# Strassen over 12 instead of 8 of 16 chunks in the projections of a streaming attention layer, with two operand sums held in DRAM

## The chip, the core and the metric

The kernel runs on one core of a Trainium2 chip. The metric is the device time of one execution in microseconds, as the median of the runs.

## What is computed

One layer for two request groups, 592 tokens in all (16 meta tokens, 512 of a new stream, 64 of a running one): a combined input projection, two kinds of attention in 8 head pairs each, gates, an output projection, and a layer norm.

```python
def in_proj(h, w_in, b_f):
    z = jnp.einsum('bld,dc->blc', h, w_in)          # d = 2048
    fq, fk, fv, fg, ff, sq, sk, sv, sg = jnp.split(z, idx, axis=-1)
    lf = jax.nn.log_sigmoid((ff + b_f).astype(jnp.float32))

def mix_prompt(h, w_in, b_f, sinks, rel_bias, w_out):
    fq, fk, fv, fg, lf, sq, sk, sv, sg = in_proj(h, w_in, b_f)
    fo = fox_prompt(fq, fk, fv, lf) * jax.nn.silu(fg)
    so = swa_prompt(sq, sk, sv, sinks, rel_bias) * jax.nn.silu(sg)
    out = jnp.einsum('blc,cd->bld', jnp.concatenate([fo, so], axis=-1), w_out)

hp = layer_norm(ALPHA * hp + out_p, ln_g[l], ln_b[l])
```

`mix_sample` does the same for the running stream with cached keys and values. Everything is float32 in and out.

## The kernel before

**Precision.** A float32 operand is split in a high part (ScalarE's copy to the type fp32r) and a low part (VectorE's subtraction). A product is three matmuls: high by high, high by low, low by high.

**Tiles.** The input projection has 52 output tiles of 128 columns; their inner dimension of 2048 is 16 chunks of 128. x lies in SBUF as `xh` and `xl`, in two halves of 296 tokens (`HALF`), "early" and "late". Two tiles make a duo, which is one step: values and gates ("vg"), queries and keys ("qk"), or gates and queries ("gq"). Duo 0 is done plainly in the opening, duos 1 to 25 are the steps.

**Strassen.** In a step the 2 by 2 blocks are (two tiles) by (two halves of the tokens), with the inner dimension split in `first_x` and `second_x` of `CUT` = 4 chunks each. Seven products (`block_product`) take the place of eight; the other eight chunks are done plainly (`plain`). Three sums of x (numbers 7, 6 and 3, high and low, `sum7_high` and so on) are made once in the opening and stay in SBUF; a fourth, the difference of two late blocks, replaces the first chunks of `xh`, `xl`. The sums of weights are made anew in each step, for the next one: `make_seven`, `make_five`, `make_six`, and `make_four` within the step. Tile 1's and tile 0's weights come in `FRONT` (the 2 x `CUT` chunks) and `BACK`.

**Units and order.** A step is 15 units of 12 matmuls each (`UNITS`, function `unit`), 180 in all. Units 0, 1, 2, 3, 6, 7, 10 are the products; 4, 5 plain work of tile 0, early; 8, 9 of tile 1, early; 11, 12 of tile 0, late; 13, 14 of tile 1, late. The order on every engine is written by hand: each of `tensor`, `scalar`, `vector` walks the same list of places s (15 for each duo of a `Stretch`) and has its own table of what comes at which unit. Attention of the pair before is put between the units by `score_at`, `turn_at` and `value_at`: for each of 5 query tiles the scores (PE), row terms and maximum (DVE, `scores`), exp (ACT, `probabilities`), reciprocal (DVE), scaling (ACT, `scale_rows`), transposes (PE, `turn`), their copy (ACT, `keep_turned`), values (PE, `values`). A first stretch has duo 1 alone; then come stretches of two duos with one pair of attention, and six of one "gq" duo with one pair each. Engines wait on semaphores in the order of their list, so what stands behind a waiting instruction waits too.

**Evacuation.** `keep_first` (ACT) copies product 0; `take_six`, `take_seven`, `take_five` (DVE) build partial results; `join` adds them to a PSUM bank and `evacuate` and `split` make the high and low parts of q and k or the silu of the gates. A bank is free for the next step when `join` has read it (`corner_summed`, `side_summed`, `top_summed`, `bottom_summed`).

**DMAs.** SyncE's queue loads the weights of the next step: its two `FRONT` parts after `right_low` and `four_made`, `BACK` after `back_low`. GpSimd's queue stores keys, values and gated results, loads the cached ones, and copies the relative bias: `copy_bias` writes 128 copies of a row per head (`rel_copies`), so that `load_bias` can read it shifted.

**Opening.** The matmuls of duo 0 run while x arrives; ScalarE and VectorE split it, then VectorE makes the sums, the front parts and weight sums of duo 1, the forget gates (`gate_inputs`, `gate_ones`, then in step 1 a reciprocal, the logs and the running sums) and the silus of duo 0.

**End.** After duo 25 come 16 tiles of the output projection, whose operands are reloaded from `mix_rows` in parts (`MIX_PARTS`), and the layer norm.

## Time and profile before

| what | value |
|---|---|
| median of 3 runs | 1019.48 us (1019.35 to 1020.27) |
| profiled execution, its time | 1019.1 us |
| profiled execution, its span | 1017.6 us |
| mean granted TensorE clock | 0.996 of full |
| busy: TensorE, VectorE, ScalarE, GpSimd | 998.6, 715.2, 531.7, 81.5 us |
| DMA moved | 115.06 MB, 113 GB/s |
| step of a two-duo stretch, twice | 59.7 us |
| step of a gq duo | 31.4 us |

A busy time is the union of an engine's instructions. "PEld" is TensorE's weight load, which overlaps the matmuls. A chain row gives the start, the length and the work that the end of the program followed from; an "x36" behind it is the number of instructions merged.

### The profile page before, as it was taken

How to read it: one execution, taken by the hardware profiler on the slowest of the kernel's cores; microseconds unless marked ns; L12 is line 12 of the kernel's file. 1: busy time of each engine (PE TensorE's matmuls, PEld its weight loads, DVE VectorE, ACT ScalarE, POOL GpSimd, SP SyncE). 2: the span in 40 equal slices, each digit the busy share in tenths (PEclk: the TensorE clock that was granted, in tenths of full speed). 3: DMA queues.
4: the chain of work that ended last, by engine and by line, in shares of the span. 5: the costliest groups of instructions: out<-in, count | busy, mean ns of one | idle time of the engine just before them, and what ended most of it. 6: DMA issues, size and time to landing. Idle time of an engine off the chain costs nothing.

```text
span 1017.6 us, 20277 instructions
## 1 busy us (share of the span) xinstructions
PE 998.6 (98%) x7283; PEld 937.3 (92%) x7283; DVE 715.2 (70%) x1423; ACT 531.7 (52%) x1217; POOL 81.5 (8%) x156
## 2 busy tenths in 40 slices
PE   9999999999999999999999999999999999999995
PEld 6899999999999999999999999999999888888884
DVE  6988686776868677686767787668787655141685
ACT  5556465565645556464655676556677562111400
POOL 1620101001010100001010000000000000000000
PEclk9999999999999999999999999999999999999998
DMA  9142333223233323234321222231226443222423
GB/s 347 57 134 100 117 112 130 90 96 108 94 125 110 126 67 103 98 106 140 111 95 60 91 81 98 98 105 56 85 82 249 173 175 104 83 82 82 166 68 118
DMA packets 36258, 115.06 MB, mean 113 GB/s; under 512 B 9312, under 2 KB 9728, under 8 KB 33584
## 3 DMA queue, kind: packets, MB, share of 16 engines
q1 hardware_dynamic: 24208, 87.00, 24.8%
q0 software_dynamic: 11856, 27.14, 7.9%
q8 instruction: 31, 0.51, 0.2%
q10 hardware_dynamic: 144, 0.26, 0.1%
q14 instruction: 19, 0.16, 0.1%
HBM read 99.31 MB, written 18.29 MB: 116 GB/s over the span
## 4 chain that ended last, share of the span: by engine, by line
PE 86%; DVE 6%; DMA 4%; issue 2%; ACT 2%; SPq 1%; DVEq 0%; ACTq 0%
PE ps L1642 28%; PE ps L1652 25%; PE ps L1895 20%; PE ps L1860 5%; PE ps L1834 4%; DMA w_raw<-in_w_all 2%; PE ps L1818 2%; PE ps L1817 2%; DMA x_raw<-in_xT 2%; DVE wl L1118 1%; DVE tb L1295 1%; PE ps L1880 1%; SPq L582 0%; PE ps L1838 0%; ACT pt L961 0%
## 5 line engine op out<-in xcount | busy, mean ns | idle before, releaser
L1642 PE MATMUL ps<-xh,wh 128*128 128x296 f32 (+1 forms) x860 | 258.8, 301 | 0.2 <-DVE xl L1366 0.2
L1642 PE MATMUL ps<-xh,wl 128*128 128x296 f32 (+1 forms) x860 | 254.8, 296 | 0.0
L1642 PE MATMUL ps<-xl,wh 128*128 128x296 f32 (+1 forms) x860 | 254.6, 296 | 0.0
L1895 PE MATMUL ps<-wh,mix_parts 128*128 128x512 f32 x576 | 184.1, 390 | 0.0
L1642 PEld LDWEIGHTS ps<-xh,wh 128*128 128x128 f32 x860 | 161.8, 188 | 3.8 <-DVE xl L1366 1.8
L1642 PEld LDWEIGHTS ps<-xl,wh 128*128 128x128 f32 x860 | 161.9, 188 | 0.0
L1642 PEld LDWEIGHTS ps<-xh,wl 128*128 128x128 f32 x860 | 161.5, 188 | 0.0
L1118 DVE TENSOR_TENSOR wl<-w_raw,wh 128x1024 fp32r<-128x1024 f32 (+1 forms) x150 | 143.0, 953 | 19.8 <-ACT wh L853 8.5
L939 ACT ACTIVATE tb<-tb,small 128x256 f32<-128x256 f32 (+5 forms) x160 | 81.3, 508 | 92.2 <-DVE small L1314 64.2
L1895 PEld LDWEIGHTS ps<-wh,mix_parts 128*128 128x128 f32 x576 | 108.2, 188 | 22.3
L1895 PE MATMUL ps<-wl,mix_parts 128*128 128x512 f32 x320 | 124.5, 389 | 0.0
L1652 PE MATMUL ps<-xh,wh 128*128 128x296 f32 x400 | 121.4, 304 | 2.0 <-ACT first_part L891 1.4
L1652 PE MATMUL ps<-xl,wh 128*128 128x296 f32 x400 | 119.2, 298 | 0.0
L1652 PE MATMUL ps<-xh,wl 128*128 128x296 f32 x400 | 119.1, 298 | 0.0
L1652 PE MATMUL ps<-sum_high,wh 128*128 128x296 f32 x300 | 92.1, 307 | 1.2 <-DVE kT L1224 1.2
L1652 PE MATMUL ps<-sum_high,wl 128*128 128x296 f32 x300 | 89.7, 299 | 0.0
L1652 PE MATMUL ps<-sum_low,wh 128*128 128x296 f32 x300 | 89.6, 299 | 0.0
L1114 DVE TENSOR_TENSOR wl<-w_raw,wh 128x1024 fp32r<-128x1024 f32 x32 | 38.1, 1222 | 68.9 <-ACT wh L841 68.8
L1652 PEld LDWEIGHTS ps<-xh,wh 128*128 128x128 f32 x400 | 75.2, 188 | 2.6 <-ACT first_part L891 1.6
L951 ACT ACTIVATE tb<-tb,small 128x256 f32<-128x256 f32 (+4 forms) x160 | 71.7, 495 | 9.8 <-DVE small L1329 9.8
L1652 PEld LDWEIGHTS ps<-xl,wh 128*128 128x128 f32 x400 | 75.4, 189 | 0.0
L1652 PEld LDWEIGHTS ps<-xh,wl 128*128 128x128 f32 x400 | 75.2, 188 | 0.0
(198 smaller groups left out, 1737.3 us busy)
## 6 DMA issues: line engine op xcount, KB each, us to landing
w_raw<-in_w_all SPq DMA_DIRECT2D x106, 512.0 KB, 4.5
w_raw<-in_w_all SPq DMA_DIRECT2D x14, 1024.0 KB, 4.8
cbc<-c_rows POOLq DMA_DIRECT2D x16, 360.0 KB, 4.1
x_raw<-in_xT SPq DMA_DIRECT2D x7, 592.0 KB, 11.7
rows<-in_x_p POOLq DMA_DIRECT2D x4, 1024.0 KB, 5.2
out_y_p<-rows SPq DMA_DIRECT2D x16, 256.0 KB, 2.5
mix_rows<-mixT POOLq DMA_DIRECT2D x14, 288.0 KB, 2.4
rel_copies<-rel_rows POOLq DMA_DIRECT2D x8, 384.0 KB, 10.5
```

Of the source, the lines that this page charges most:

```text
L939: nc.scalar.activation(t, t, ACT.Exp, bias=nm, accum_out=total[:, i % 3, head:head + 1]).then_inc(exp_done, 1)
L951: nc.scalar.activation(row, row, ACT.Copy, scale=recip[:, i % 3, head:head + 1]).then_inc(scaled, 1)
L1114: nc.vector.tensor_tensor(wl[slot][:, a], w_raw[slot % 2][:, a], wh[slot][:, a].bitcast(F32), ALU.subtract).then_inc(w_low, 1)
L1118: nc.vector.tensor_tensor(low, raw, high.bitcast(F32), ALU.subtract).then_inc(done, 1)
L1295: ins = nc.vector.scalar_tensor_tensor(out=rows_[:, head, a:b], in0=st.score_out(ps, head, piece, b - a), scalar=cqp[:, i, head:head + 1], ...
L1642: ins = nc.tensor.matmul(ps[:, bank, result(tile, h)], a[f][:, w], b[:, ko, first:first + width], start=(ko == n_first and i == 0), stop=( ...
L1652: ins = nc.tensor.matmul(ps[:, bank, 0:HALF], a[:, w], b[:, j, :], start=(start and j == 0 and i == 0), stop=(stop and j == CUT - 1 and i ...
L1817: nc.tensor.matmul(out, queries, k2[:, head, a:b], start=True, stop=False)
L1818: ins = nc.tensor.matmul(out, queries, k_low[:, head, a:b], start=False, stop=True)
L1834: ins = nc.tensor.transpose(st.turn_out(ps, head, j), tb[:, i % SLOTS, head, first:first + P], ident[:])
L1860: ins = nc.tensor.matmul(ps[head_rows(head), bank, at:at + q], v_nat[:, block_, HD * head:HD * head + HD], moving[:, head, 0:q], start=(j ...
L1895: ins = nc.tensor.matmul(ps[:, bank, :], a, b[slot][:, w], start=(ko == 0 and i == 0), stop=(ko == KO - 1 and i == len(products) - 1))
```

## The change

`CUT` becomes 6 chunks, so Strassen covers 12 of 16 and `REST`, 2 chunks a unit, is done plainly. A step is 29 pieces of 6 matmuls (`PIECES`, `UNIT_PIECES`), and every table of every engine is written anew in pieces; the distances of attention double with them (`lag`). Units 8 to 12 change their order: the late half of tile 0 (product 8, plain 9 and 10) now comes before the plain work of tile 1's early half (11, 12). The sums 6 and 3 no longer both lie in SBUF: they share `sum_both`. In the opening sum 6 is stored to DRAM (`sum_rows`), sum 3 is made in place of an x block and split in step 1 (`last_sum`), then stored too; in every later step SyncE fetches sum 6 after unit 7 and sum 3 after unit 1. Before the first front loads of step 2 SyncE waits for both stores. The front loads of duo 1 wait for `w_low` 3 and 4 instead of 1 and 2. The silus of duo 0 use other buffers, the gate terms lie elsewhere with one tile fewer, and the logarithm moves into step 1. `rel_copies` holds 32 copies a head instead of 128, and `load_bias` reads it in four parts.

```diff
 UNITS = 15
+UNIT_PIECES = [3, 3, 3, 3, 1, 1, 3, 3, 3, 1, 1, 1, 1, 1, 1]
+PIECES = sum(UNIT_PIECES)
 DUOS = PROJ_TILES // 2
-CUT = KO // 4
+CUT = 3 * KO // 8
+REST = (KO - 2 * CUT) // 2
-GATES_TURNED_AT, V_FIRST_AT = 11, 14
+GATES_TURNED_AT, V_FIRST_AT = 22, 28
-BIAS_COPIES = FOX_PAIRS
+BIAS_COPIES, COPIES = FOX_PAIRS, CHUNK // 2
-MIX_PARTS = [(0, 2), (2, 5), (5, 8), (8, 12), (12, 14)]
+MIX_PARTS = [(0, 2), (2, 6), (6, 9), (9, 12), (12, 14)]
...
         elif len(duos) == 2:
-            score = [3 * i + 3 for i in range(5)]
+            score = [6 * i + 6 for i in range(5)]
         else:
-            score = [2 * i + 1 for i in range(5)]
-        turn = [x + 4 for x in score]
+            score = [4 * i + 2 for i in range(5)]
+        self.lag = 1 if final else 2
+        turn = [x + 4 * self.lag for x in score]
...
-        sum7_high, sum7_low, sum6_high, sum6_low, sum3_high, sum3_low = (
-            sb(f"sum{n}", [P, CUT, HALF], F32R) for n in ("7_high", "7_low", "6_high", "6_low", "3_high", "3_low"))
+        sum7_high, sum7_low = (sb(f"sum{n}", [P, CUT, HALF], F32R) for n in ("7_high", "7_low"))
+        sum_both = sb("sum_both", [P, 2, CUT, HALF], F32)
+        both_high, both_low = (sum_both[:, i, :, :].bitcast(F32R) for i in range(2))
...
@@ block.sync
             for f in range(2):
-                sp.wait_ge(w_low, f + 1)
+                sp.wait_ge(w_low, f + 3)
                 load_part(1, f, FRONT, front_loaded)
             for f in range(2):
-                sp.wait_ge(w_low, f + 3)
                 load_part(1, f, BACK, back_loaded)
+            sp.wait_ge(sum_low, 2)
+            sp.dma_start(sum_rows[0], sum_both[:].rearrange("p a b c -> p (a b c)")).then_inc(sums_stored, 16)
             sp.wait_ge(back_low[0], 1)
             load_part(2, 0, BACK, back_loaded)
+            sp.wait_ge(sum_low, 4)
+            sp.dma_start(sum_rows[1], sum_both[:].rearrange("p a b c -> p (a b c)")).then_inc(sums_stored, 16)
+            sp.wait_ge(sums_stored, 32)
...
-                sp.wait_ge(*((four_made, d) if f == 0 else (right_low, d)))
+                sp.wait_ge(*((four_made, d) if f == 0 else (five_low, d)))
...
+            def load_sums(i, used, loaded):
+                sp.wait_ge(unit_done, used)
+                sp.dma_start(sum_both[:].rearrange("p a b c -> p (a b c)"), sum_rows[i]).then_inc(loaded, 16)
+            def load_three(d):
+                load_sums(1, UNITS * (d - 1) + 2, three_loaded)
+            def load_duo(d):
+                load_next_front(d, 0)
+                load_next_front(d, 1)
+                load_next_back(d)
+                load_sums(0, UNITS * (d - 1) + 8, six_loaded)
+                sp.wait_ge(back_low[0], d + 1)
+                load_part(d + 2, 0, BACK, back_loaded)
...
@@ block.scalar, per place
+                        if r == 3:
                             keep_first(st, k)
+                        if r == 4:
                             five_part(d, (unit_done, st.after(k, 0)))
+                        if r == 6:
                             right_part(d, (unit_done, st.after(k, 1)))
+                        if st.first and r == 7:
+                            last_sum(st)
+                        if r == 24 and not last:
+                            seven_part(d + 1, (unit_done, st.after(k, 8)))
+                            six_part(d + 1, (unit_done, st.after(k, 7)))
...
+                    if inside and r == 18 and not last:
+                        front_parts(d + 1, (unit_done, st.after(k, 6)))
...
@@ block.vector, per place
+                        if r == 6:
                             take_six(st, k)
+                            five_part(d)
+                        if r == 8:
+                            right_part(d)
+                        if r == 9:
                             take_seven(st, k)
+                            make_four(d, (unit_done, st.after(k, 2)))
+                        if r == 14:
                             join(st, k, 0, 0)
+                        if r == 17:
                             take_five(st, k)
+                        if r == 25:
+                            join(st, k, 0, 1)
+                        if r == 27:
                             join(st, k, 1, 0)
...
+                            if r == 20:
                                 front_parts(d + 1)
+                            if r == 21:
                                 make_seven(d + 1, (unit_done, st.after(k, 7)))
                                 make_five(d + 1)
+                            if r == 22:
                                 make_six(d + 1)
+                            if r == 25:
                                 seven_part(d + 1)
                                 six_part(d + 1)
+                            if r == 28:
                                 back_parts(d + 1, 0)
...
@@ block.tensor, unit()
                 elif u == 1:
+                            pe.wait_ge(six_loaded, 16 * d - 16)
...
                 elif u == 7:
+                            pe.wait_ge(three_loaded, 16 * d - 16)
```

## Rows read from the trace of the kernel before

**Rows 1.** The page: engines, busy us (share of the span) xinstructions.

```profile
PE 998.6 (98%) x7283; PEld 937.3 (92%) x7283; DVE 715.2 (70%) x1423; ACT 531.7 (52%) x1217; POOL 81.5 (8%) x156
```

**Rows 2.** Windows in two stretches: length, busy of each engine, clock, DMA share, GB/s.

```profile
166.00:226.00 60.00, 60.00 (x486) 58.97 (x486) 44.72 (x93) 33.83 (x78) 4.90 (x8) 1.00 0.32 107
...
584.90:616.30 31.40, 31.40 (x261) 30.48 (x260) 24.81 (x58) 21.97 (x61) 1.77 (x3) 1.00 0.24 82
```

**Rows 3.** Chain that ended last, 221 to 284 us: start, length, work.

```profile
230.49 3.09 PE ps L1642 x24
...
249.52 4.89 PE ps L1652 x36
```

**Rows 4.** Opening: windows; chain; VectorE and SyncE in order of time.

```profile
26.70:45.00 18.30, 17.66 (x142) 16.23 (x140) 17.74 (x22) 12.25 (x18) 15.22 (x32) 1.00 0.03 10
45.00:73.40 28.40, 25.86 (x189) 25.15 (x190) 24.72 (x46) 12.48 (x24) 7.15 (x16) 1.00 0.41 136
...
26.81 1.31 DVE raw L1378
...
72.01 1.93 PE ps L1652 x12
...
50.19 0.67 DVE L1152 TENSOR_TENSOR w_sum<-w_raw 128x512 f32<-128x512 f32 x1
...
72.47 0.95 DVE L1260 TENSOR_TENSOR k_low<-kT,k 64x296 fp32r<-64x296 f32 x2 [0.52 <-ACT k L917]
...
50.49 2.01 SPq L596 DMA_DIRECT2D w_raw<-in_w_all  x3
```

**Rows 5.** Groups by line and shape: busy us, mean ns, idle before.

```profile
L1118 DVE TENSOR_TENSOR wl<-w_raw,wh 128x1024 fp32r<-128x1024 f32 x75 | 91.5, 1221 | 16.5 <-ACT wh L853 8.5 <-ACT wh L847 8.0
L853 ACT ACTIVATE wh<-w_raw 128x1024 fp32r<-128x1024 f32 x50 | 52.4, 1047 | 0.2
L1118 DVE TENSOR_TENSOR wl<-w_raw,wh 128x512 fp32r<-128x512 f32 x75 | 51.4, 686 | 3.3
L877 ACT ACTIVATE wh<-w_raw 128x512 fp32r<-128x512 f32 x25 | 15.4, 617 | 0.6 <-PE ps L1652 0.6
```

**Rows 6.** Windows while x loads, and after the last matmul; columns as in rows 2.

```profile
14.00:20.00 6.00, 6.00 (x50) 5.09 (x53) 5.06 (x4) 5.12 (x5) 0.00 (x0) 1.00 1.03 424
...
1008.00:1012.00 4.00, 0.00 (x0) 0.00 (x0) 3.83 (x9) 0.29 (x1) 0.00 (x0) 0.76 0.00 0
1012.00:1017.00 5.00, 0.00 (x0) 0.00 (x0) 2.67 (x5) 0.00 (x0) 0.00 (x0) 0.50 0.58 210
```

**Rows 7.** DMA issues: KB, us to landing; weight loads, 90 to 400 us.

```profile
w_raw<-in_w_all SPq DMA_DIRECT2D x14, 1024.0 KB, 4.8
...
mix_raw<-mix_rows SPq DMA_DIRECT2D x1, 1152.0 KB, 9.3
...
DMA to landing us min/median/max: 3.2/4.9/7.4
```

**Rows 8.** Chain near 379 us; rel_copies, 370 to 392 us; whole chain, one place.

```profile
379.10 7.40 DMA w_raw<-in_w_all
...
DMA to landing us min/median/max: 11.5/11.5/11.5
...
274.92 2.12 PE ps L1860 x36
...
334.59 2.12 PE ps L1860 x36
...
516.41 2.12 PE ps L1860 x36
```

**Rows 9.** One gq step in order of time: VectorE, ScalarE, TensorE.

```profile
584.58 0.69 DVE L1301 TENSOR_TENSOR tb<-ps,bias 128x512 f32<-128x512 f32 x1 [0.23 <-DVE small L1274]
...
613.56 0.47 DVE L1224 TENSOR_TENSOR last_part<-ps,last_part 128x296 f32<-128x296 f32 x1 [2.32 <-PE ps L1642]
...
607.27 0.58 ACT L961 ACTIVATE pt<-ps 128x512 f32<-128x512 f32 x1
...
607.97 1.09 PE L1860 MATMUL ps<-pt,v_nat 128*64 128x128 f32 x16
```

More of the change, by code:

```diff
@@ L153, in metas, with terms @@
     @staticmethod
+    def terms(g):
+        return 32 * g + 32
+    @staticmethod
     def metas(g, i):
@@ L191, in metas, with terms @@
     @staticmethod
+    def terms(g):
+        return 32 * FOX_PAIRS + 64 * (g - FOX_PAIRS) + 64
+    @staticmethod
     def metas(g):
@@ L216, in __init__ @@
         self.last, self.final = last, final
-        self.steps = OUT_STEPS if final else UNITS * len(duos)
+        self.steps = OUT_STEPS if final else PIECES * len(duos)
         if final:
@@ L886, in keep_first @@
                 act.wait_ge(unit_done, st.after(k, 0))
[L887 to L889 removed]
+                if not st.first:
                     act.wait_ge(bottom_summed, st.duo(k) - 1)
@@ L1042, in run @@
+                        if r == 9:
                             back_parts(d, 1, (projected[1], 2) if st.first else (unit_done, st.after(k, -1)))
-                        if u == 5:
+                        if st.first and r == 9:
+                            gate_log()
+                        if r == 12:
                             four_part(d)
-                        if u == 6:
+                        if r == 14:
                             evacuate(st, k, 0, 0)
-                        if u == 7 and not last:
-                            front_parts(d + 1, (unit_done, st.after(k, 6)))
@@ L1062, in run @@
-                        if last and u in (11, 12):
-                            act.wait_ge(unit_done, st.after(k, 10))
-                            mixed_high(u - 11)
-                    for i in st.at(st.score_at, s - 2):
+                        if r == 27 and last:
+                            weights_high(0, 0, 1, (unit_done, st.after(k, 10)), True)
+                        if last and r in (20, 23):
+                            act.wait_ge(unit_done, st.after(k, 6))
+                            mixed_high(r // 22)
@@ L1287, in scores @@
                 if i == 0:
-                    dve.wait_ge(row_terms_loaded, 32 * st.g + 32)
+                    dve.wait_ge(row_terms_loaded, st.kind.terms(st.g))
                 pieces = st.kind.score_pieces(tile)
@@ L1399, in opening_splits @@
                 for h in range(2):
-                    silu(st, h, (first_part, diff_part)[h], ps[:, 2 + h, :])
+                    silu(st, h, (mid_part, last_part)[h], ps[:, 2 + h, :])
                 dve.wait_ge(sum_made, 4)
-                dve.wait_ge(sum_high, 4)
+                dve.wait_ge(sum_high, 3)
                 low_of(xl[:, first_x, late], x_raw[:, first_x, late], xh[:, first_x, late], sum_low)
@@ L1541, in run @@
                         keep_values(st)
-                    if st.first and s == GATES_TURNED_AT - 1:
+                    if st.first and s == GATES_TURNED_AT + 1:
                         keep_gates()
@@ L1644, in plain, with block_product @@
                 return ins
-            def block_product(bank, weights, x, start, stop):
+            def block_product(piece, bank, weights, x, stop):
                 (high, low), (x_high_part, x_low_part) = weights, x
-                for j in range(CUT):
+                for j in range(2 * piece, 2 * piece + 2):
                     w = slice(j * P, (j + 1) * P)
                     for i, (a, b) in enumerate(((high, x_high_part), (high, x_low_part), (low, x_high_part))):
-                        ins = nc.tensor.matmul(ps[:, bank, 0:HALF], a[:, w], b[:, j, :], start=(start and j == 0 and i == 0),
+                        ins = nc.tensor.matmul(ps[:, bank, 0:HALF], a[:, w], b[:, j, :], start=(j == 0 and i == 0),
                                                stop=(stop and j == CUT - 1 and i == 2))
@@ L1715, in unit @@
                         pe.wait_ge(under_made, d)
-                    ins = plain(1, 1, duo[1], BOTTOM, range((u - 11) * CUT, (u - 10) * CUT), 2 * CUT)
-                ins.then_inc(unit_done, 1)
+                    ins = plain(1, 1, duo[1], BOTTOM, rest(u - 13), 2 * CUT)
+                if piece == UNIT_PIECES[u] - 1:
+                    ins.then_inc(unit_done, 1)
             def opening_products():
```

277 lines of the change are left out of this document (141 added, 136 removed).

## Prediction

> **What bounds the kernel now.** I read the table of engines first [rows 1]: TensorE is busy 998.6 of 1017.6 us, VectorE 715, ScalarE 532. The windows over single stretches follow [rows 2]: in a repeated stretch of two projection steps TensorE is busy 60.0 of 60.0 us at full clock, and in a step of one attention pair 31.4 of 31.4, VectorE 24.8 there. The reader is to see that nothing is idle on TensorE in the steps, so fewer matmuls is time at once, as long as the others keep up. The chain that ended last says the same, and it gives the price of a matmul: 36 of 296 columns in 4.89 us, 24 of 280 columns in 3.09 us [rows 3]. So 0.136 and 0.129 us each, and no gain from a busy share (each matmul's own record is 0.3 us long and overlaps the next). There is one stretch of another kind, the opening. From 26.7 to 73.4 us VectorE is busy 42.5 of 46.7 us, and the chain runs through it from its first sum of x at 26.81 to the third product of step 2, which TensorE can begin only at 72.01 [rows 4]. There VectorE is the bound.
>
> The profiled execution has a span of 1017.6 us and a time of 1019.1; the median of the runs is 1019.48. I sum against 1019.1 and add 0.4 at the end.
>
> **Matmuls removed.** Strassen's seven products cover 12 of the 16 chunks instead of 8. A step had 7 products x 4 chunks x 3 + 8 plain units x 12 = 84 + 96 = 180 matmuls; it gets 7 x 6 x 3 + 8 x 6 = 126 + 48 = 174. The products are 296 columns wide, some removed plain ones 280. In a step with one 280-column tile: 6 more of 296, 12 fewer of 280, 0.82 - 1.54 = -0.73 us. In one of the six "gq" steps (two such tiles): 18 more, 24 fewer, 2.45 - 3.09 = -0.64 us. After step 1, which I count with the opening, there are 24 steps: 18 x 0.73 + 6 x 0.64 = **-17.0 us** [rows 3].
>
> **Opening, VectorE.** The sums of x grow from 4 to 6 chunks: 1184 to 1776 elements a partition. VectorE takes 1.221 us for 1024 and 0.686 for 512 elements [rows 5], 1.045 ns an element, so 0.62 us more each. Before the second step can use its second key tile there are three sums, one difference, and four low parts (one now moved into step 1, `last_sum`): 8 x 0.62 = 4.9. The weights grow from 512 to 768 elements in nine operations of a step (4 sums, 5 low parts, +0.27 each), the front low part from 1024 to 1536 (+0.53), and two back parts shrink (-0.53 each): +1.9 a step. Preparing step 1 has five of the nine, the front and one back part, +1.3; step 1 itself and preparing step 2 +1.9. Together +8.1 us on an engine that has 4.2 idle us there, many of them answers of ScalarE that stay (`k_low` behind `k`, 0.52 [rows 4]). What is given back is at most the 1.6 us that the third product of step 2 now starts later (after 36 matmuls, not 24). The other moves (silus into `mid_part` and `last_part`, Ln later, gate terms in other memory) only change order on the two engines; I cost them at nothing, because VectorE's queue of work covers them, and at 0.5 us if it doesn't.
>
> **Opening, SyncE.** This is an added wait. The two sums go to DRAM from one buffer; the second store can be issued when `last_sum`'s low part is done, and SyncE then waits for both stores before it issues any front load of step 2. Before, those were issued at 50.49 us, 2.0 us in all [rows 4], behind `four_made`'s kind of wait alone. That time I lay out from `make_four`, which ended at 50.9 before: +4.3 for seven larger operations on x, +2.1 for the weights, +0.8 for the tanh of the silus, which ScalarE now does later, -1.3 for the third sum's low part and -1.9 for the gates' reciprocal, which both now come after, and 2.0 for `last_sum` itself: 56.9. A store of 1776 KB: no row shows its size. The high rate in the trace is 424 GB/s [rows 6], so 4.3 us, on top of some 2.0 that a 512 KB load needs beyond its bytes (3.2 us at best [rows 7]): 6.3. From the slow end, a fetch of 1152 KB in pieces of 2304 bytes took 9.3 us [rows 7], so 14.3. Its 14-KB rows per partition are nearest to the weights' (1024 KB in 4.8), so I take 7. Fronts are issued at 64, the first lands near 68.4, ScalarE copies it to 69.9, and VectorE, otherwise ready for it at 66.5, stands for 3.4 us. Behind it wait the seven, five and six parts of step 2, its joins and through them TensorE. The Trainium skill, in "DMA: Bandwidth & Descriptors", section "Anatomy of one DMA — SWDGE (gpsimd) path", gives 2.0 us plus bytes over 436 GB/s for one kind of queue; that would be 6.2 us for the store, and the sum would be 0.8 us lower. Opening: 8.1 + 3.4 = **+11.5 us**, between 6.5 (wait covered, 1.6 given back) and 19 (the slow store).
>
> **Stalls that go.** ScalarE waited for a weight load that took 7.40 us and TensorE stood at the turn behind it; beside it ran `rel_copies`, 384 KB in many small rows, landing after 11.5 us [rows 8]. It now carries 96 KB. The same place of the loop is 59.67 us apart in an undisturbed iteration (274.92 to 334.59), and the next three take 181.82 instead of 179.01 [rows 8]: **-2.8 us**, and 0 if the cause was another. Step 2 lost about 1 us on two turns, of which I expect half again: **-0.5**.
>
> **The pair steps, where cover runs out.** VectorE's +1.9 a step lies beside TensorE's work: in a two-step stretch 44.7 of 60 us become 48.5 in one that should last 58.2. In a gq step 24.8 of 31.4 become 26.7 of 30.8, and here the order decides. Laid out by hand, each duration that of the same operation in this step before, with the larger sizes of [rows 5]: scores 0 at 2.7 us of the step (584.58 [rows 9], the step's first matmul at 581.9), max by 4.3, exp to 5.7, the low of five to 7.4, scores 1 to 8.5, right, seven and four to 10.6, scores 2 to 12.8, exp 14.2, scores 3 to 16.5, take five 18.6, scores 4 to 20.9; ScalarE's front part (1536 columns, 1.5 us) to 21.4, VectorE's low to 23.1, seven and five to 24.9, the last reciprocal to 25.2, six to 26.1. ScalarE then has scale 4 and `keep_turned` 3 by 26.7, just when TensorE asks for it at the values before turn 4 (in the kernel before it was copied by 607.85 and asked for at 607.97 [rows 9], 0.12 us of room). The rest (two joins, seven and six lows, silu, q low, back low) ends at 32.2, 1.4 us after the next step began, so its scores start 1 us late. Counting round the loop gives some 31.8 us: 26.7 of work and 5 of answers between VectorE and ScalarE that order can't hide (6.6 idle before, 2.32 of them in one piece that the longer work uses up [rows 9]). Against 30.8 of TensorE that is 1 us in a second and 1.2 in a third step of a row; the first of a row starts on time. Two rows of three: **+4 us**, between 0 (answers overlap better) and 8.
>
> **The fetches.** Each of the two sums comes back, 1776 KB twice a step. The third's has units 2 to 6 as cover, 11 pieces x 0.82 = 9.0 us without any attention; the sixth's has 12, 9.8 us. At 7 us both are hidden: 0. On SyncE, the third's fetch stands before the front loads, whose `four_made` comes at 10.6 anyway; the fronts land by 17 and are wanted at 20. Fifty transfers of 1.82 MB more: the 107 GB/s of a two-step stretch [rows 2] become some 235, where 424 were reached [rows 6]. Bias loads in four quarters on GpSimd's queue: +2 issues of 0.6 us on an engine busy 8%, nothing. The last step's split loads and the final stage are unchanged in work: nothing, 0.5 at worst.
>
> **Sum.** 1019.1 - 17.0 + 11.5 - 2.8 - 0.5 + 4.0 = 1014.3, and with the 0.4 to the median 1014.7, given as 1015.
>
> **Rivals.**
> (B) The cover holds. SyncE's wait is hidden and 1.6 us given back in the opening (6.5), no pair step waits: 1019.1 - 17.0 + 6.5 - 3.3 + 0.4 = 1005.7, say 1006. For it: two-step stretches show no idle TensorE and VectorE at 75% [rows 2]. Against: VectorE's queue in the opening is simply longer.
> (C) Slower: a fetch is not hidden. It decides from 9.0 us of landing in a step without attention, 10.9 where a gq or two-step stretch gives 0.17 us more a piece. At the slow end, 14.3 us, each of 24 steps waits 3.4 us: 1015 + 82 = 1097; one microsecond late is 1039. For it: `mix_raw` and late `x` rows are that slow [rows 7]. Against: they stood behind other traffic or had short pieces.
> (D) The same: every step with attention, not only gq ones, loses 0.3 us on a turn that has no room (two-step stretches): 1015 + 18 x 0.3 = 1020.
> (E) TensorE's clock. It is 1.00 in every window but the end: 0.76 and then 0.50 in the microseconds after its last matmul at 1007 [rows 6], that is, at 1.2 of 2.4 GHz once it has nothing to do. My chain has two waits of TensorE of about 4 us each between 70 and 86 us. If the clock drops in each and stays low for as long again, 4 us of matmuls take 8, twice: 1015 + 8 = 1023, or 1019 for one. The Trainium skill says in "TensorE: Matmul & The Clock Gate", section "What's actually happening", that the slow clock is the default and activity lifts it, which would make the second of these waits dearer; the trace agrees as far as its tail goes.
> That the change doesn't do what it says is no real rival: the matmul count follows from `CUT`.
>
> **Chances and range.** Forecast 0.43 (1010 to 1019), B 0.26, D 0.13, E 0.08, C 0.10. A measurement of this kernel tells about 0.2%, 2 us, from no change. Faster is under 1017.4: nearly all of B and 0.41 of the forecast, 0.67. Within: 0.02 + 0.11 of D + 0.05 of E = 0.18. Slower: 0.15. The range goes from 1004 (B with the store at 6.3) to 1021 (D and the nearer half of E); C stays outside.
>
> **What would show it.** 174 matmul records a step, all at 0.136. TensorE reaching the score of step 2 (73.8 us before) at about 85: at 80 the wait on the stores was hidden, past 90 they were slow. A front load of step 2 issued at 64. Fetches landing in 7 us. Gq steps at 30.8, 31.8, 32.0; all 30.8 is B, and two-step stretches at 58.2 rule D out. VectorE 44 us busier in all, ScalarE some 18. The prediction is wrong if a step waits for `sum_both`, or if the opening grows by less than 6.

## The result, and the profile after

The changed kernel takes 1075.55 us (median of four runs, 1073.44 to 1077.62) against 1019.58 for the kernel before: a ratio of 1.0548, with a 95% interval of 1.0535 to 1.056. It is 5.5% slower. The prediction was 1015 us, range 1004 to 1021, with 0.67 on faster. The profiled execution took 1077.6 us, its span is 1076.1.

The engine table and the waits of TensorE, by what released them (total us, times, longest), of the changed kernel:

```profile
PE 1012.6 (94%) x7133; PEld 942.5 (88%) x7133; DVE 764.0 (71%) x1423; ACT 547.1 (51%) x1217; POOL 88.8 (8%) x172
```

```profile
PE ps L1889 <- DVE k_low L1311: 24.1, 10, 3.5
PE ps L1932 <- ACT pt L997: 16.2, 8, 2.8
```

Against [rows 1] there are 150 fewer matmuls and TensorE is busy 14 us longer, in a span 58.5 us longer. VectorE is busy 764.0 us (+48.8; the forecast was +44) and ScalarE 547.1 (+15.4; 18). Two waits stand out that the kernel before doesn't have at all: for the low part of the keys, 24.1 us in ten places, and for the copy of transposed probabilities, 16.2 us in eight.

The windows over one two-duo stretch and one gq step, as in [rows 2], and then four single microseconds (length, busy of TensorE, weight load, VectorE, ScalarE, GpSimd, clock, DMA share, GB/s):

```profile
236.10:298.80 62.70, 60.42 (x472) 58.80 (x471) 48.00 (x91) 34.67 (x77) 4.49 (x8) 0.97 0.59 213
615.90:651.50 35.60, 33.01 (x254) 32.02 (x254) 26.39 (x57) 22.32 (x61) 2.73 (x5) 0.93 0.49 172
...
270.00:271.00 1.00, 0.00 (x0) 0.00 (x0) 0.74 (x2) 0.95 (x3) 0.54 (x1) 1.00 0.34 98
271.00:272.00 1.00, 0.81 (x3) 0.63 (x4) 0.48 (x3) 0.95 (x4) 0.43 (x1) 0.82 1.57 377
272.00:273.00 1.00, 1.00 (x6) 1.00 (x6) 0.65 (x2) 1.00 (x2) 0.26 (x1) 0.50 0.55 199
...
275.00:276.00 1.00, 1.00 (x9) 1.00 (x8) 0.93 (x3) 0.00 (x0) 0.00 (x0) 0.97 0.87 346
```

The stretch that was to last 58.2 us lasts 62.7. VectorE is busy 48.0 of it, where 48.5 were forecast: the amount of work was right, and TensorE stands all the same. Nothing in the busy shares, 77% for VectorE, shows why. In the last rows TensorE's granted clock is 1.00 while it stands, at 270, and 0.50, that is 1.2 instead of 2.4 GHz, at 272 when it works again; at 275 it is back.

Step by step, read from the last matmul of each fifteenth unit, in both traces:

| part | before | expected by the sum | after | lost beside the sum |
|---|---|---|---|---|
| opening with steps 1 and 2 | 101.6 | 111.9 | 111.2 | -0.7 |
| qk steps of stretches, 7, each | 28.16 | 27.4 | 27.41 | 0 |
| vg steps of stretches, 7, each | 31.5 to 31.6 (three at 32.1 to 33.0) | 30.8 | 34.4 to 35.5 | 29.4 |
| gq steps, second and third of a row, 4 | 31.4 | 31.8 to 32.0 | 35.2 to 35.7 | 14.2 |
| gq steps, first of a row, 2 | 31.4 | 30.8 | 40.4 and 40.6 | 19.4 |

The removed matmuls are there: a qk step, which has no wait in either kernel, is 0.75 us shorter (0.73 in the sum). The opening came out as summed in its total, though not in its parts (e5_wait_moved). The rest, 63 us, is the miss, and it sits in the steps with attention.

**Where a vg step stands.** The chain of the changed kernel through the turn from a qk to a vg step (start, length, work; lines left out at "..."):

```profile
253.38 0.04 ACT wh L885
...
254.78 0.29 ACT k L966
...
256.68 1.76 DVE wl L1167
258.44 0.88 DVE w_sum L1183
...
262.59 0.95 DVE wl L1167
...
265.59 0.48 DVE kT L1275
...
267.98 0.64 ACT wh L891
...
269.75 0.46 ACT k L953
...
270.23 0.46 DVE k_low L1311
...
271.19 0.39 PE ps L1889
...
273.34 5.72 PE ps L1708 x36
```

The chain leaves TensorE at 253.38, where unit 6 has ended and frees the front weights, and comes back to it at 271.19, at the first score of the next pair. In between nothing waits for a transfer; it is one row of work on ScalarE and VectorE: the high and low part of 1536 front weights, the cached keys of the next pair (254.78), sums seven and five, the values' copies, sum six, two low parts, q, one half of the keys, the back weights, the other half, and its low part. The kernel before has the same chain in less time and with more cover. Four rows of its trace, of TensorE, VectorE (two) and TensorE, in order of time:

```profile
234.91 0.30 PE L1652 MATMUL ps<-xh,wl 128*128 128x296 f32 x1
```

```profile
240.73 0.47 DVE L1224 TENSOR_TENSOR kT<-ps,diff_part 128x296 f32<-128x296 f32 x1 [1.00 <-PE ps L1642]
...
251.15 0.96 DVE L1260 TENSOR_TENSOR k_low<-kT,k 64x296 fp32r<-64x296 f32 x2 [0.52 <-ACT k L917]
```

```profile
254.25 0.28 PE L1817 MATMUL ps<-k,q 128*128 128x272 f32 x1
```

Unit 6's last matmul starts at 234.91, the last low part of the keys ends at 252.11, 17.2 us later, and TensorE asks for it only at 254.25, 19.3 us after unit 6. In the changed kernel unit 6's last matmul starts at 253.05, TensorE arrives at score 0 at about 269.0, and the keys are there at 271.2: cover 15.9 instead of 19.3 us, chain 18.1 instead of 17.2. (The 17.2 us hold 1.0 us in which VectorE waits for TensorE, at 240.73; the changed chain has no such wait, so the work in it grew by more than 0.9 us.) A product is 18 matmuls now and was 12, so unit 6, the last that needs the front, ends later in the step, and fewer matmuls lie between it and the score.

**Where a gq step stands.** ScalarE and then TensorE at the end of the second gq step, in order of time (in brackets the idle time before, and what ended it):

```profile
643.63 0.57 ACT L997 ACTIVATE pt<-ps 128x512 f32<-128x512 f32 x1
644.10 0.83 ACT L897 ACTIVATE wh<-w_sum 128x768 fp32r<-128x768 f32 x1
...
647.83 0.89 ACT L948 ACTIVATE q<-diff_part 64x280 fp32r<-64x280 f32 x2 [1.83 <-DVE diff_part L1275]
648.75 0.63 ACT L891 ACTIVATE wh<-w_raw 128x512 fp32r<-128x512 f32 x1
649.29 0.58 ACT L997 ACTIVATE pt<-ps 128x512 f32<-128x512 f32 x1
```

```profile
645.10 0.66 PE L1906 MATMUL ps<-ident,tb 128*128 128x128 f32 x4
...
649.92 0.45 PE L1932 MATMUL ps<-pt,v_nat 128*64 128x64 f32 x8 [2.59 <-ACT pt L997]
```

The turn of the last tile is done at 645.8. Its copy (649.29) stands in ScalarE's list behind q's early half (647.83), which waits 1.83 us for VectorE's join, and TensorE waits 2.59 us for it. Then the clock halves here too: 0.93 in the mean of the step.

### The profile page after: what moved, and what is told of

It reads as the page before. It is cut to its first block, busy times and chain, and to the rows that moved or that the text cites. A ratio compares the mean times of both kernels' runs of the same rounds, so it can differ in the third digit from the quotient of the medians.

```text
span 1076.1 us, 20084 instructions
## 1 busy us (share of the span) xinstructions
PE 1012.6 (94%) x7133; PEld 942.5 (88%) x7133; DVE 764.0 (71%) x1423; ACT 547.1 (51%) x1217; POOL 88.8 (8%) x172
## 4 chain that ended last, share of the span: by engine, by line
PE 60%; DVE 14%; issue 9%; ACT 8%; DMA 2%; DVEq 1%; ACTq 0%; SPq 0%
PE ps L1708 24%; PE ps L1967 19%; PE ps L1698 7%; DVE wl L1167 4%; PE ps L1932 4%; PE ps L1906 3%; ACT k L953 2%; PE ps L1889 2%; DMA w_raw<-in_w_all 2%; PE ps L1890 2%; DVE w_sum L1183 1%; ACT wh L885 1%; ACT k L966 1%; ACT wh L891 1%; DVE kT L1275 1%
## 5 line engine op out<-in xcount | busy, mean ns | idle before, releaser
L1708 PE MATMUL ps<-xh,wh 128*128 128x296 f32 x600 | 186.9, 311 | 4.4 <-DVE wl L1167 3.2
L1708 PE MATMUL ps<-xh,wl 128*128 128x296 f32 x600 | 182.0, 303 | 0.0
L1708 PE MATMUL ps<-xl,wh 128*128 128x296 f32 x600 | 181.5, 303 | 0.0
L1167 DVE TENSOR_TENSOR wl<-w_raw,wh 128x1536 fp32r<-128x1536 f32 (+1 forms) x150 | 149.8, 999 | 30.1 <-ACT wh L891 12.2
L1698 PE MATMUL ps<-xh,wh 128*128 128x296 f32 (+1 forms) x460 | 142.0, 309 | 0.4 <-DVE xl L1417 0.4
L1698 PE MATMUL ps<-xl,wh 128*128 128x296 f32 (+1 forms) x460 | 138.8, 302 | 0.0
L1698 PE MATMUL ps<-xh,wl 128*128 128x296 f32 (+1 forms) x460 | 138.6, 301 | 0.0
L1708 PE MATMUL ps<-sum_both,wh 128*128 128x296 f32 x600 | 126.0, 301 | 2.1 <-DVE wl L1167 1.1
L1708 PEld LDWEIGHTS ps<-xh,wh 128*128 128x128 f32 x600 | 116.0, 193 | 5.8 <-DVE first_part L1275 3.4
L1708 PEld LDWEIGHTS ps<-xl,wh 128*128 128x128 f32 x600 | 115.9, 193 | 0.0
L1708 PEld LDWEIGHTS ps<-xh,wl 128*128 128x128 f32 x600 | 115.4, 192 | 0.0
L1708 PEld LDWEIGHTS ps<-sum_both,wh 128*128 128x128 f32 x600 | 96.8, 188 | 4.3 <-issue 3.3
L1708 PE MATMUL ps<-sum_both,wl 128*128 128x296 f32 x300 | 89.6, 299 | 0.0
```

The lines of the kernel that those rows point to most:

```text
L1167: nc.vector.tensor_tensor(low, raw, high.bitcast(F32), ALU.subtract).then_inc(done, 1)
L1698: ins = nc.tensor.matmul(ps[:, bank, result(tile, h)], a[f][:, w], b[:, ko, first:first + width], start=(ko == n_first and i == 0), stop=( ...
L1708: ins = nc.tensor.matmul(ps[:, bank, 0:HALF], a[:, w], b[:, j, :], start=(j == 0 and i == 0), stop=(stop and j == CUT - 1 and i == 2))
```

## Experiments

Times are of one execution each, except in b1_copies, and differences are taken from the profiled execution of the changed kernel, 1077.6 us; from its median they are 2 us smaller. The changed kernel's own executions lie 4 us apart, so differences under about 3 us aren't read from times but from the steps in the trace. In e6_small and e8_no_fetch part of the computation is left out, as their expectations say.

**e1_score_late: all scores 3 pieces later.**

```diff
-            score = [6 * i + 6 for i in range(5)]
+            score = [6 * i + 9 for i in range(5)]
```

> One edit to the changed kernel: in two-duo stretches all five scores (and with them turns and values) come 3 pieces later, score 0 at piece 9 instead of 6. Its own profile shows TensorE waiting 2.2 to 2.6 us for k_low before score 0 in each of the 8 such stretches. Theory W (a window became too short: from the end of unit 6, which frees the front weights, to score 0 TensorE has 14.7 us of matmuls where it had 18.0, and VectorE and ScalarE have more to do in it): 3 pieces are 2.45 us, the wait goes, and with it the stretch of halved clock behind it, 2.4 to 3.4 us each, 1077.6 - 8 x 2.9 = about 1054. Rival T (VectorE has simply too much work per stretch): the wait only moves to a later turn or value, 1075 to 1078.

Measured: 1086.8 us, 9 slower. Neither theory said that. The vg step fell from 35.5 to 30.6 us, so the wait for the keys did go, but the qk step rose from 27.4 to 34.3:

```profile
PE ps L1952 <- DVE mixT L1394: 18.7, 7, 2.8
PE ps L1932 <- ACT pt L997: 16.1, 8, 2.8
PE ps L1906 <- ACT tb L987: 14.3, 17, 1.6
...
PE ps L1889 <- DVE k_low L1311: 3.8, 2, 2.0
```

The values' transposes (L1952) now wait up to 2.8 us for the gating of the previous pair, and turns (L1906) for ScalarE. The attention of the old pair had been pushed into the same window. So a later score doesn't make cover; it puts more work into the place that has none. The vanished wait fits the cause that theory W names; its forecast of 1054 us was missed, and my remedy was wrong.

**e2_keep_early: the last copy of a gq step ahead of q.**

```diff
-                    for i in st.at(st.turn_at, s - st.lag):
+                    for i in st.at(st.turn_at, s - (1 if len(st.duos) == 1 else st.lag)):
```

> One edit to the changed kernel: in gq steps ScalarE copies each transposed block one piece earlier in its list, so the last one stands ahead of the evacuation of q's early half instead of behind it. The profile shows TensorE waiting 2.6 to 2.8 us for that copy at the end of each gq step, while ScalarE's list stands at q, which waits for VectorE's join. Theory W/list: the wait goes in all 6 gq steps, and the halved clock behind it (1.3 to 2 us): 6 x 4 = 24 us, about 1054. Rival T (VectorE bounds the step): no more than 1 us a step, 1072 or above.

Measured: 1058.4 us, 19 less. The gq steps take 36.6, 32.4, 32.5 and 36.8, 32.4, 31.2 us, and the wait for `pt` is 1.4 us in all instead of 16.2. So a place in ScalarE's list cost 19 us: 21 in the gq steps, less 3 that the stage behind the last step now takes longer, where TensorE waits 2.1 us ahead of a score and then runs at half clock for 3.4. What is left, 32.4, is what my layout of VectorE and ScalarE had given for such a step (31.8 to 32.0).

**e3_both: the two together.**

> Both edits. Theory W: the gains add, 1077.6 - 23 - 24 = about 1031. Rival T: 1070 or above; if they add only in part, the gq step after a two-duo stretch is where they meet.

Measured: 1072.6 us, 14 less than e1_score_late, where 1031 was expected from the failed first edit. The second edit keeps most of its worth beside the first.

**e4_order: the order of units as before.** The lists of ScalarE and VectorE follow.

```diff
+ORDER = [0, 1, 2, 3, 4, 5, 6, 7, 11, 12, 8, 9, 10, 13, 14]
-PIECE_OF = [(u, j) for u, n in enumerate(UNIT_PIECES) for j in range(n)]
+PIECE_OF = [(u, j) for u in ORDER for j in range(UNIT_PIECES[u])]
```

> The changed kernel with the order of units as in the kernel before: tile 1's plain early half ahead of the last product and tile 0's late half, still CUT 6 and 29 pieces. Rival O (the moved half is the cause: tile 1's two halves of keys or queries are now evacuated in one bunch at the step's end): two-duo stretches fall from 62 to 58.2 us and gq steps from 35.4 to about 31, so about 1020. Theory W (the sum of the work between unit 6's end and score 0 is the same in either order): the two-duo stretches stay at 61 to 62.5 us; gq steps may win 0 to 2 us as q's early half no longer stands before the last copy: 1063 to 1077.

Measured: 1081.5 us. Rival O falls: the order didn't make the loss. The stretches stay at 63 to 65 us, and the wait has only changed its name:

```profile
PE ps L1709 <- DVE mid_part L1276: 31.9, 10, 3.4
PE ps L1933 <- ACT pt L998: 17.5, 12, 1.8
```

Now the next step's first product waits up to 3.4 us for bank TOP, whose join now comes at the step's end. The moved half made room for that bank, at the price of the keys.

**e5_wait_moved: SyncE's wait for the stores behind the front loads.**

```diff
-            sp.wait_ge(sums_stored, 32)
...
                 load_next_back(d)
+                sp.wait_ge(sums_stored, 32)
                 load_sums(0, UNITS * (d - 1) + 8, six_loaded)
```

> One edit to the changed kernel: SyncE waits for the two stores of the sums ahead of its first fetch of sum 6, not ahead of the front loads of step 2. In the profile of the changed kernel the chain runs through the second store (56.17 to 62.06 us) and the front load (to 66.57), and VectorE stands from 65.6 to 68.1. If that chain is the price of the wait, VectorE goes on at once and the score of step 2 begins 2 to 3 us earlier (83.75 us before), in all -2.5 us. If VectorE's own work is the whole price of the opening, nothing: 0 to -0.5 us. (One look can tell this only by the start of that score.)

Measured: 1072.8 us, and the score of step 2 begins at 83.59 instead of 83.75. The fronts are issued at 56.98 instead of 62.08, and it is worth 0.2 us. In the changed kernel the chain does run where I had put it:

```profile
56.17 5.89 DMA sum_rows<-sum_both
...
62.08 4.50 DMA w_raw<-in_w_all
...
66.59 1.49 ACT wh L885
...
83.75 0.42 PE ps L1889
```

but the load that is issued earlier doesn't land earlier. ScalarE's copy of the first front part in the changed kernel and then in e5_wait_moved, each with its wait for the load:

```profile
66.59 1.48 ACT L885 ACTIVATE wh<-w_raw 128x1536 fp32r<-128x1536 f32 x1 [4.59 <-DMA w_raw<-in_w_all]
```

```profile
66.44 1.48 ACT L885 ACTIVATE wh<-w_raw 128x1536 fp32r<-128x1536 f32 x1 [3.98 <-DMA w_raw<-in_w_all]
```

Issued 0.4 us behind the store of 1776 KB instead of after it, the front part takes 9.4 us to land instead of 4.5, and the store 6.8 instead of 5.9. So the 3.4 us of the sum are no price of SyncE's wait: whether the load waits for the store or shares the way with it, it lands at the same time. e12_seven, which has the same edit, repeats it (issued at 56.38, 9.47 us).

TensorE's clock fell in the opening as well. Two windows of the changed kernel:

```profile
63.50:70.20 6.70, 6.70 (x31) 6.37 (x30) 4.13 (x7) 1.48 (x1) 2.33 (x4) 0.50 0.95 361
84.00:87.30 3.30, 3.30 (x15) 3.20 (x15) 2.56 (x6) 3.26 (x5) 0.15 (x1) 0.50 0.97 337
```

Both stand behind a wait, of 3.16 us (to 62.09) and 3.48 us (to 83.75). In e5_wait_moved the clock is at half from 61.6 to 71.6, and 18 matmuls take 4.78 us where 2.45 is their time at full clock (e5_wait_moved, a row of its chain):

```profile
62.54 4.78 PE ps L1708 x18
```

The score of step 2 comes at the same time all the same, so the first fall costs nothing that shows. The second fall is missing in e5_wait_moved, and step 2 takes 35.2 us there instead of 36.6; in e8_no_fetch, where it falls, step 2 takes 36.7. By these, about 1 us of the opening's time is the clock's, as an estimate.

**e6_small: the sizes of before in the window.** From step 2 on, 8 of 12 chunks of the front, and 4 of 6 of three sums and of two of their parts.

```diff
-                low_of(wl[0][:, FRONT], w_raw[0][:, FRONT], wh[0][:, FRONT], front_low)
+                f = FRONT if isinstance(d, int) and d == 1 else slice(0, 8 * P)
+                low_of(wl[0][:, f], w_raw[0][:, f], wh[0][:, f], front_low)
...
-                low_of(wl[1][:, B], w_sum[:, A], wh[1][:, B], seven_low)
+                A4, B4 = (A, B) if isinstance(d, int) and d == 1 else (slice(0, 4 * P), slice(CUT_LEN, CUT_LEN + 4 * P))
+                low_of(wl[1][:, B4], w_sum[:, A4], wh[1][:, B4], seven_low)
```

> The changed kernel with the high and low part of the front weights over 8 of the 12 chunks, and sums seven, five and six, and the high and low parts of seven and six over 4 of 6 chunks, from step 2 on: as large as in the kernel before (so a third of the products' chunks gets stale weights). VectorE has 1.9 us less a step in the window between unit 6's end and score 0, ScalarE 1.0 us. Everything else is left. If those sizes (terms of the sum of the prediction) make the waits: two-duo stretches 62.3 to 59.0, gq steps by 2 to 3 us less: 1077.6 - 8 x 3.3 - 6 x 2.5 = about 1036. If the new places of the work make them, sizes aside: no more than 10 us less, 1067 or above.

Measured: 1043.7 us, 34 less. Stretches take 59.7 us, gq steps 33.5 to 35.9. Keys are waited for 5.2 us in all instead of 24.1. The 1.9 us of VectorE and 1.0 of ScalarE, which I had laid "beside TensorE's work", cost 1.7 to 3.2 us in each vg step, since they lie in the chain and their absence also keeps the clock up.

**e7_fill: matmuls in place of the waits.**

```diff
+                    if len(st.duos) == 1 and st.kind and not st.last and s == st.value_at[4]:
+                        fill(20)
...
+                    if len(st.duos) == 2 and s == st.score_at[0]:
+                        fill(18)
```

> The changed kernel with 18 extra matmuls of 272 columns (2.3 us at full clock) just ahead of score 0 in the two-duo stretches, and 20 ahead of the last values in gq steps (all but the last), where TensorE otherwise stands 2.2 to 2.8 us; they read x, write a bank that the next score overwrites, and nobody uses them. Nothing that the waits depend on is changed. If the halved clock behind the waits has a price of its own, it goes: stretches of 62.8 us become 61.9, gq steps lose 1 to 2 us less, mean clock from 0.974 to about 0.99, in all -10 to -16 us, 1062 to 1067. If the slow matmuls were hidden (VectorE and ScalarE set the pace anyway), the time stays at 1075 to 1078 though the clock is up.

Measured: 1066.0 us, 12 less, with TensorE busy 16.6 us more. The same windows, over one stretch and one gq step:

```profile
233.70:295.50 61.80, 61.53 (x490) 59.53 (x489) 47.93 (x91) 34.70 (x77) 4.50 (x8) 1.00 0.59 216
643.70:677.40 33.70, 33.37 (x274) 32.28 (x274) 26.39 (x57) 22.36 (x61) 2.72 (x5) 1.00 0.53 185
```

The clock is 1.00 in both, the mean over the run 0.994 instead of 0.974. The steps that had lasted 34.4 us stay at 34.4, and those of 35.4 come down to it; in the trace of the changed kernel the former are the ones in which the clock had stayed up. So a wait of 2.2 to 2.5 us sometimes takes the clock down afterwards and sometimes doesn't, and it then costs 1 us more in a vg step and 1 to 2 in a gq step: 12 of the 58 us, a little of it in step 2. The two falls that are left in this execution are in the opening and in the last gq step, which has no extra matmuls.

**e8_no_fetch: no sums fetched.**

```diff
-                sp.dma_start(sum_both[:].rearrange("p a b c -> p (a b c)"), sum_rows[i]).then_inc(loaded, 16)
+                sp.dma_start(sum_both[:, 0, 0, 0:16], sum_rows[i][:, 0:16]).then_inc(loaded, 16)
```

> The changed kernel with each fetch of a sum cut to 16 of its 3552 columns (8 KB instead of 1776 KB), same waits and same places (so products with sums 6 and 3 use a stale sum). The prediction had the fetches at nothing: 8.3 us to landing against 9.0 us of cover. If that holds, and the traffic of 1.8 MB twice a step slows nothing else, 1075 to 1077. If the fronts' loads, which land 6.3 us after issue beside the fetch, hold ScalarE's copy back in each step: 1 to 2 us a step less, about 1050.

Measured: 1072.5 us, within 1 us of the changed kernel's fastest run, and the waits for keys and `pt` are 23.6 and 16.1 us, as before. The 87 MB of fetches cost nothing that shows. In the changed kernel they land in time:

```profile
sum_both<-sum_rows SPq DMA_DIRECT2D x48, 1776.0 KB, 8.3
w_raw<-in_w_all SPq DMA_DIRECT2D x52, 768.0 KB, 6.3
```

**e9_tighter and e10_earlier: only the first scores later.** Both with the edits of e2_keep_early and e5_wait_moved, and the scores at [9, 14, 19, 24, 30] and [8, 13, 18, 23, 28].

> The early copy in gq steps (as in e2_keep_early), the moved wait (as in e5_wait_moved), and in two-duo stretches scores at pieces 9, 14, 19, 24, 30 instead of 6, 12, 18, 24, 30: only the first ones are later, so that the gating and the values' copies at the stretch's end stay where they were (in e1_score_late they came later, and TensorE stood 2.7 us for them in each stretch). Theory W: score 0 then finds its keys, and no new wait is made: 8 stretches at 58.5 to 59 us instead of 62 to 63, 1058.4 - 8 x 3.5 - 2.5 = about 1028. If VectorE has no room for tiles 5 pieces apart in a step, a turn or a value waits instead: 1045 to 1058.

> As e9_tighter with scores at pieces 8, 13, 18, 23, 28: the attention ends 2 pieces earlier, ahead of the weights' preparation, score 0 is 1 piece earlier. Theory W: score 0 waits up to 0.8 us, the end has more room: 1026 to 1036. If tiles 5 pieces apart are too close: the same loss as in e9_tighter.

Measured: 1063.7 and 1056.2 us, against 1058.4 for e2_keep_early alone. Both miss. TensorE's waits in the second of them:

```profile
PE ps L1708 <- DVE kT L1275: 6.6, 8, 2.0
PE ps L1906 <- ACT tb L987: 6.1, 10, 0.8
PE ps L1906 <- ACT pt_meta L999: 5.1, 8, 0.7
```

Product 2 (L1708) now waits for bank BOTTOM, which the last join of the keys frees: that join is in the same chain, and with the score out of its way TensorE comes to the bank before it. And tiles 5 pieces apart are too close for ScalarE's scaling and copying. Two more uses of the same window.

**e11_cached: 1.9 us taken out of the window.** On top of e2_keep_early:

```diff
-        self.cached_at = self.steps - (10 if kind else 4)
+        self.cached_at = self.steps - (16 if kind else 4)
```

> e2_keep_early plus one number: the cached keys are split at piece 42 of a two-duo stretch (and 13 of a gq step that has them) instead of 48, where VectorE stands 3.2 us for TensorE anyway. In the profile this work (1.25 us of ScalarE, 0.59 of VectorE) lies in the chain between unit 6's end and score 0. Theory W (that chain sets score 0): 1.9 us leave it, the wait of 2.4 us falls to 0.5, and the halved clock behind it goes: 8 stretches by 2.4 to 2.9 us, the first gq step of each row too: 1058.4 - 20 to 28 = 1030 to 1038. If not that chain but VectorE's total or the buffers set the pace: 1055 or above.

Measured: 1041.1 us, 17 less than e2_keep_early. The same amount of work, moved from 254.78 in the chain above to a place where VectorE stands 3.2 us for TensorE in any case:

```profile
231.90:292.10 60.20, 59.12 (x472) 57.29 (x471) 47.97 (x91) 34.70 (x77) 4.50 (x8) 1.00 0.62 222
595.50:627.90 32.40, 31.94 (x254) 29.83 (x254) 26.24 (x57) 22.31 (x62) 2.72 (x5) 1.00 0.55 192
```

```profile
PE ps L1889 <- DVE k_low L1311: 11.8, 10, 3.5
```

VectorE's busy time is the same 48.0 us, and the stretch is 2.5 us shorter, with the clock at 1.00. Each wait for the keys in these stretches is 0.9 us now, where it was 2.2; the longest in the row above, 3.5 us, is the opening's, which this edit doesn't reach.

**e12_seven and e13_eight: score 0 one and two pieces later, with that work moved.** Scores at [7, 12, 18, 24, 30] and [8, 13, 18, 24, 30], and the moved wait.

> e11_cached with the moved wait of e5_wait_moved and scores at 7, 12, 18, 24, 30: score 0 one piece (0.82 us) later, tile 1's one earlier relative to it. If what is left of the wait (1.08 us) is the same chain, it falls to 0.3 us with nothing in its place: 8 x 0.8 and a little clock, 1041 - 8 = about 1033. If bank BOTTOM or a turn now waits instead, as in e9_tighter and e10_earlier: 1038 to 1043.

> The same with scores at 8, 13, 18, 24, 30. Same chain: the wait is gone, 1041 - 10 = about 1031. With the bank (product 2 cannot start before the last join has read BOTTOM, also in that chain): product 2 waits about 0.3 us and turns of tiles 5 pieces apart some tenths, 1034 to 1043.

Measured: 1036.3 and 1045.4 us. The first is 4.8 us less than e11_cached (the wait for the keys is 2.1 us in all, mean clock 0.996), but not all of it is the piece's: the seven vg steps fall from 32.8 to 32.5 us, 2.4 us together, and 2.2 us come from the opening with steps 1 and 2 (109.3 instead of 111.5 us), where this run has the moved wait and a clock of 1.00 from 60 to 90 us, while e11_cached is at half clock for 13 us there. With two pieces the bank and the turns wait again, more than I had given them. So what is left of the wait is the same chain, and score 0 has one place, between the keys and the bank.

**b1_copies: the kernel before, with 32 copies of a bias row.** Five executions. The same edit as in the change, with the four loads.

```diff
-        rel_copies = nc.dram_tensor("rel_copies", [N_HEADS, P, REL], F32, kind="Internal").ap()
+        rel_copies = nc.dram_tensor("rel_copies", [N_HEADS, COPIES, REL], F32, kind="Internal").ap()
```

> The kernel before with one part of the change alone: 32 copies of a bias row instead of 128, read in four parts. The prediction gave -2.8 us to this: its profile has three weight loads that land after 7.4 us beside a copy of 384 KB. If the copy is the cause: ratio 0.9973. If the loads are late for another reason: 1.000.

Measured: 1015.3 us against 1018.9, ratio 0.9965 (0.9951 to 0.9979). The weight loads between 90 and 400 us, which took up to 7.4 us in [rows 7], now land so:

```profile
DMA to landing us min/median/max: 3.1/4.0/5.5
```

and all vg steps from the second stretch on take 31.5 to 31.6 us. This is the fastest kernel of all that ran, faster than both given ones.

## Why the prediction was wrong

**Right.** The matmuls removed: -0.75 us in an undisturbed step, where -0.73 stood. The opening: the sum put the score of step 2 at about 85 us, it came at 83.75; opening with steps 1 and 2 took 0.7 us less than summed. That it fits so well is luck in part: the 3.4 us for SyncE's wait are not that wait's, since the load issued without it takes 9.4 us (e5_wait_moved), and about 1 us is half clock, which the sum didn't have. The stall beside `rel_copies`: -2.8 forecast, -3.6 measured alone in b1_copies. The fetches at nothing: landing was 8.3 us in the median, 7.2 to 10.1 between 90 and 600 us, where I took 7; no wait of TensorE is put down to the load of `sum_both`, and e8_no_fetch confirms it. Rival C, the one on the slower side, named a mechanism that didn't occur. VectorE's and ScalarE's added work came to 49 and 15 us, where 44 and 18 stood; the 44 is 23 steps of 1.9 us alone, and with the opening's 8.1 the sum's own terms give 52. The lower end of the range had no sum behind it: in B the wait for the stores is covered, so a faster store can't make B shorter.

**The step that failed.** "VectorE's +1.9 a step lies beside TensorE's work: in a two-step stretch 44.7 of 60 us become 48.5 in one that should last 58.2." I took a busy share over 60 us as cover. The work doesn't lie anywhere in the stretch: most of it lies between two fixed points, the end of unit 6 and the next score 0 (or bank TOP or BOTTOM). There the kernel before had 19.3 us of TensorE's work over a chain of 17.2, so 2.1 us of room in the stretch shown; the prediction never read that number, though the trace held it. The change took 3.4 us of the cover (larger products move unit 6 back) and lengthened the chain by 0.9; e6_small shows the sizes to be over half of what is lost. The term was 0 and measured 29.4 us over seven vg steps. Of these 15.6 us are the seven waits for the keys and about 4 the half clock behind four of them; the other 10, 1.4 a step, are in gaps too short for a row of their own, and no run takes them apart. Rival D had a loss in these stretches too, but at a turn (a transpose) and at 0.3 us each, with no row behind the price; it came at the score, and a vg step lost 3.6 to 4.8.

**The gq steps.** +4 was forecast for the six, it is 38 beside the removed matmuls. The layout by hand was good to half a microsecond once one thing is mended: e2_keep_early has 32.4 us where 31.8 to 32.0 stood. What it missed is the last line of ScalarE's list. I followed the copy of tile 3, and put down "the rest" at 32.2 as if nothing on TensorE waited for it; the copy of tile 4 stood in that rest. The first step of a row I took to start on time; it has the keys' wait of a vg step, and a second score only 4 pieces behind, and lost 9.6 us.

**The clock.** Rival E had two waits of 4 us in the opening and a price of 4 us each. One is there, 3.5 us to 83.75; the other that occurred, 3.2 us, ends at 62.09, in step 1. The clock fell behind both, but the first fall cost nothing that shows and the second about 1 us. What the rival lacked are the waits of 2.2 to 2.8 us in the steps, because the sum had no such waits. e7_fill gives the clock's size, 12 us, which is a price on top of the stalls.

**Shares of the 58 us.** The runs overlap, so they don't add up: 19 us go with a place in ScalarE's list (e2_keep_early), 17 more with the cached keys' place (e11_cached), 2.4 with one piece of the first score (e12_seven, in its steps); or 34 with the sizes (e6_small); or 12 with the clock alone (e7_fill). What remains in e12_seven against the kernel before, 17 us, comes from the opening with steps 1 and 2 (7.7 us more than before), from vg steps of 32.5 us (1.7 more than the sum has), from gq steps that take 4 us (the first of a row) and mostly 1.6 us (later ones) more than TensorE's work, and from the stage behind the last step (3.0 us more), less what the removed matmuls save. Whether another order of VectorE's list would win these back wasn't tried.

## What to carry to other kernels

A busy share says whether an engine can do its work in a loop, not whether it does it in time: find the event that releases a helper's work and the event that needs it, and set the chain's length against the cover between the two, in the kernel before, as the room that a change may use up. When a block of the bound engine grows, its last reader of a buffer moves back, and the window behind it shrinks, without any added work. And of each engine's list read the last entries of a step too: what stands behind a waiting one is needed by somebody.

## What the runs showed of the hardware

- TensorE's clock can drop after a wait of only 2.2 us. Behind the wait that ends at 271.19 it is granted at 1.00 during the wait, falls to 0.50 within 1 us after the work goes on, and stays there some 3 us (windows above); behind the wait of the same length that ends at 333.96 it doesn't fall at all. In the kernel before, whose longest wait of TensorE is 1.6 us, it doesn't fall until the last matmul is done. 18 to 20 otherwise useless matmuls in each wait held it at 1.00 in every stretch and gq step that had them, and were worth 12 us (e7_fill). The Trainium skill, "TensorE: Matmul & The Clock Gate", section "What's actually happening", describes a slow clock that activity lifts. This trace agrees: the clock is back at 0.97 at 275, with TensorE busy since 271.19. The price comes after the wait, on matmuls that wait for nothing.
- 1776 KB to or from DRAM, in rows of 14 KB a partition, took 5.9 us as a store (56.17 above) and 7.2 to 10.1 as a fetch beside other loads.
- A load of 768 KB issued 0.4 us behind that store took 9.4 us to land, and 4.5 when it was issued after the store had landed (e5_wait_moved and the changed kernel): removing a wait between two transfers gained 0.2 us.
- A copy of 384 KB in short pieces beside the loads went with landings of up to 7.4 us for a 512 KB weight load; with 96 KB the slowest is 5.5 (b1_copies), and the kernel is 3.6 us faster.
